# Two-layer hybrid diffusion block in one kernel: the last token strip is computed in blocks among the first steps of the mixers, and the second query pair is prepared in pieces between attention units

## What is computed

```python
u = adaln(x, norm1_w, shift, scale) @ w_in          # 2056 columns: pooling, SSD (Mamba-2), attention
pooled = pool_mixer(u[:, :256])                     # window means minus self, a small matmul
y_ssd  = ssd_bidirectional(u[:, 256:1288])          # chunks of 128 tokens, a state carried over the chunks, both ways
q, k, v = attn_split(u[:, 1288:])                   # 4 query heads and 2 key/value heads of 128
q, k = rmsnorm(q) * q_norm_w, rmsnorm(k) * k_norm_w
q, k = apply_axial_rope(q), apply_axial_rope(k)     # on the latent tokens
y_att = softmax(q @ k.T / sqrt(128)) @ v
x = x + gate * (concat([pooled, y_ssd, y_att]) @ w_out)
```

## Time and profile before

| what | value |
|---|---|
| median of 3 runs | 1600.78 us (1600.17 to 1602.5) |
| profiled execution | 1601.48 us |
| its span | 1599.7 us |
| TensorE busy | 1542.1 us, 96% |
| VectorE busy | 876.7 us, 55% |
| ScalarE busy | 592.0 us, 37% |
| GpSimd busy | 138.9 us, 9% |

### The profile page before, as it was taken

How to read it: one execution, slowest core, us unless ns; L and a number is a source line. 1 busy time by engine, 2 the same in 40 slices (tenths; PEclk the granted TensorE clock), 3 DMA queues, 4 the chain that set the end, 5 groups by cost and what they waited for, 6 DMA issues and landing times.

```text
span 1599.7 us, 22334 instructions
## 1 busy us (share of the span) xinstructions
PE 1542.1 (96%) x9086; PEld 1392.9 (87%) x9086; DVE 876.7 (55%) x1192; ACT 592.0 (37%) x896; POOL 138.9 (9%) x150
## 2 busy tenths in 40 slices
PE   6999879999999999999999999997999999999999
PEld 4899758899999999999999997985888788888887
DVE  4678777645765545555544367457656433333333
ACT  6634546634521111221122345354645322222223
POOL 0330132011000000000000024014101000000000
PEclk9999979999999999999999999998999999999999
DMA  9655300022444333333331123320013233333322
GB/s 370 177 171 170 86 1 2 1 67 90 134 145 131 112 126 132 106 131 132 122 115 56 50 79 84 81 69 1 1 53 93 86 92 99 92 92 97 91 85 83
DMA packets 204220, 156.05 MB, mean 98 GB/s; under 512 B 8740, under 2 KB 189804, under 8 KB 204012
## 3 DMA queue, kind: packets, MB, share of 16 engines
q1 hardware_dynamic: 202700, 150.16, 30.4%
q10 hardware_dynamic: 1440, 4.78, 0.8%
HBM read 151.52 MB, written 2.10 MB: 96 GB/s over the span
## 4 chain that ended last, share of the span: by engine, by line
PE 86%; DVE 7%; ACT 3%; issue 2%; POOL 1%; DMA 1%; SPq 0%; POOLq 0%; DVEq 0%; ACTq 0%
PE banks L1788 69%; PE banks L1906 5%; PE banks L2025 3%; PE banks L1932 2%; PE banks L2002 1%; DVE mod_sum L1249 1%; PE banks L2039 1%; DVE w_lo L1224 1%; PE banks L2063 1%; DVE nrm L1326 1%; PE banks L2003 1%; DVE h_lo L1320 1%; ACT nrm L885 1%; PE banks L1740 0%; PE banks L1727 0%
## 5 line engine op out<-in xcount | busy, mean ns | idle before, releaser
L1224 DVE TENSOR_TENSOR w_lo<-raw,w_hi 128x1056 fp32r<-128x1056 f32 x184 | 245.0, 1332 | 303.9 <-ACT w_hi L832 303.1
L1788 PE MATMUL banks<-h_hi,w_hi 128*128 128x384 f32 (+3 forms) x1296 | 386.4, 356 | 10.5 <-DVE h_lo L1320 5.4
L1788 PE MATMUL banks<-h_lo,w_hi 128*128 128x384 f32 (+3 forms) x1296 | 382.0, 353 | 0.0
L1788 PE MATMUL banks<-h_hi,w_lo 128*128 128x384 f32 (+3 forms) x1296 | 381.7, 353 | 0.0
L832 ACT ACTIVATE w_hi<-raw 128x1056 fp32r<-128x1056 f32 x184 | 198.5, 1079 | 247.2 <-PE banks L1788 227.1
L1788 PEld LDWEIGHTS banks<-h_hi,w_hi 128*128 128x128 f32 x1296 | 235.0, 188 | 40.9 <-DVE h_lo L1320 11.9
L1788 PEld LDWEIGHTS banks<-h_hi,w_lo 128*128 128x128 f32 x1296 | 237.2, 188 | 16.7
L1788 PEld LDWEIGHTS banks<-h_lo,w_hi 128*128 128x128 f32 x1296 | 237.0, 188 | 15.8
L1788 PE MATMUL banks<-g_hi,w_hi 128*128 128x384 f32 (+1 forms) x528 | 160.0, 357 | 0.0
L1788 PE MATMUL banks<-g_hi,w_lo 128*128 128x384 f32 (+1 forms) x528 | 159.1, 355 | 0.0
L1249 DVE SCALAR_TENSOR_TENSOR mod_sum<-mod_ring,cond,mod_sum 128x1024 f32<-128x1024 f32 x126 | 158.1, 1296 | 1.4
(11 more groups left out here) (209 smaller groups left out, 1871.0 us busy)
## 6 DMA issues: line engine op xcount, KB each, us to landing
raw<-in_w_dram SPq DMA_DIRECT2D x120, 512.0 KB, 3.8
mod_ring<-in_w_mod_dram SPq DMA_DIRECT2D x96, 512.0 KB, 4.8
raw<-in_w_in_dram SPq DMA_DIRECT2D x32, 512.0 KB, 4.8
raw<-in_w_out_dram SPq DMA_DIRECT2D x16, 512.0 KB, 3.7
raw<-in_w_dram SPq DMA_DIRECT2D x16, 384.0 KB, 3.1
x_in<-in_x_dram ACTq DMA_DIRECT2D x4, 512.0 KB, 7.4
out_dram<-x_out SPq DMA_DIRECT2D x8, 256.0 KB, 2.3
inv_n<-in_count_dram ACTq DMA_DIRECT2D x4, 400.0 KB, 3.1
```

Of the source, the lines that this page charges most:

```text
L1224: dve.tensor_tensor(w_lo[n % 2][:, :], raw[n % 4][:, :], as_f32(w_hi[n % 2][:, :]), ALU.subtract).then_inc(lo_ready, 1)
L1788: ins = pe.matmul(to(p, a, b), ws[:, w], xs(k, a, b), start=(first and q == 0), stop=(last and q == 2))
```

## The change

1. The second query pair's strip is no longer computed by `token_blocks` ahead of the mixers. It is cut into `block` events (six in layer 0, four in layer 1), each with the 24 matmuls of one block of tokens, placed among the transposes, `cs` and the first state steps. They use PSUM banks 0 and 1 in turn; the transposes now use banks 2 and 3 (one of them bank 0).
2. The transposes of the keys and of the first query head come after the last block, and the pooling matmuls after the first unit's scores. The first query pair's sum, scaling, sine and rotation are events `q01` among the blocks. The five state steps all stand in the head.
3. `x_w` moves to another address (on the ring of slabs), so that states can run before the last block; GpSimd now waits for the last modulation slab before the first `x_w` instead of before `h_prev`'s zeroes.
4. The second query pair's squares (`q23_squares`) are taken in the head, its sum in unit 0, its scaling in two halves, the sine, and the rotation's two steps in later units (`in_unit`). It gets tiles of its own (`qk_sq_last`, `rope_t_last`).
5. The SSD chunks begin at unit 1 (before: 2). The two last `mod_steps` of layer 0 and its `mod_total`/`mod_turn` are events too. Tile 16 of `w_out` is split at unit 8 (before: ahead of the mixers).

```diff
-        x_w = put("x_w", [P, 2, DIRS, 256], at=S0 + 19456)
+        x_w = put("x_w", [P, 2, DIRS, 256], at=M0 + 4 * TT * 256 + 8 * T)
...
-            ev = [("tr", "x", 0), ("tr", "x", 1), ("tr", "b", 0), ("tr", "k", 0), ("tr", "k", 1), ("cs",), ("q23", 0),
-                  ("pool", 0), ("pool", 1), ("q23", 1), ("tr", "q", 0)]
-            ev += states[:1] + [("q23", 2)] + states[1:2] + [("q23", 3)]
-            states = states[2:]
+            blocks = [("block", i, t) for i, t in enumerate(range(tok_from(l, 3), TT))]
+            ev = [("tr", "x", 0), blocks[0], ("cs",), ("q01", 0), ("tr", "x", 1), ("mod_steps",), blocks[1], ("tr", "b", 0), ("q01", 1), blocks[2]]
+            if l < DEPTH - 1:
+                ev += [("mod_total",), blocks[3], states[0], ("mod_turn",), blocks[4], states[1], ("q01", 2), states[2], ("q01", 3), blocks[5],
+                       ("tr", "k", 0), states[3], ("tr", "k", 1), ("tr", "q", 0), ("q23_squares",), states[4]]
+            else:
+                ev += [states[0], blocks[3], states[1], ("q01", 2), ("tr", "k", 0), states[2], ("q01", 3), ("tr", "k", 1), states[3],
+                       ("tr", "q", 0), ("q23_squares",), states[4]]
+            states = []
+            in_unit = {0: [("q23", 0), ("pool", 0), ("pool", 1)], 2: [("q23", 1)], 3: [("q23", 2)], 4: [("q23", 3)], 5: [("q23", 4)], 6: [("q23", 5)]}
+            if l == DEPTH - 1:
+                in_unit = {0: in_unit[0], 1: [("q23", 1)], 2: [("q23", 2), ("q23", 3)], 4: [("q23", 4)], 5: [("q23", 5)]}
+            in_unit[8] = [("w_out_tile",)]
...
+                ev += in_unit.get(u, [])
...
-                if todo and not states:
+                if todo and u:
                     last_c = todo.pop(0)
                     ev.append(("ssd", last_c))
-                for _ in range(2):
-                    if states:
-                        ev.append(states.pop(0))
...
-                for n in range(N_TOK):
+                for n in range(N_TOK - 1):
                     split_lo(base + N_FEAT + n + 1)
                     if n == 5:
                         rotate(0)
                     if l == 0:
                         biases(N_FEAT + n)
-                        mod_steps(N_FEAT + n)
+                        if n != 5:
+                            mod_steps(N_FEAT + n)
...
-                    for j in range(4):
+                    for j in range(4 if i == 0 else 2):
...
+                    elif e[0] == "block":
+                        i, t = e[1:]
+                        pe.wait_ge(tok_free, tok_count(l, 3) + (i - 1 if i >= 2 else i - 5))
+                        for half in range(2):
+                            n = base + N_FEAT + N_TOK - 2 + half
+                            pe.wait_ge(lo_ready, n + 1)
```

173 lines of the change are left out of this document (117 added, 56 removed).

## The result

The changed kernel took 1586.1 us (median of 4 runs, 1585.2 to 1588.0) against 1600.5 us before (4 runs, 1596.9 to 1602.5) in the same session: a ratio of 0.9915, 95% interval 0.9902 to 0.9929. The forecast was 1582.5 us with a range of 1573 to 1592. The profiled execution took 1585.9 us with a span of 1584.0 us; before these were 1601.5 and 1599.7 us.

What follows compares the result with a forecast made beforehand. TensorE was taken as the bound except in the two heads, idle there behind VectorE and GpSimd chains. 11.4 + 9.5 - 2 x 1.3 = 18.3 us off 1601.5 gave 1583.2, 1582.5 as median; range 1573 to 1592.

Steps and rivals of the forecast that it cites:

- The bound and the mechanism: Both heads: TensorE idles 15.7 and 10.6 us behind VectorE and GpSimd chains; blocks cover the first pair's, the second's moves out.
- Up to the first scores, layer 0: Layer 0's head: waits of 1.2 us for `w_lo` and `mod_total`, scores at 196.3, 1.4 us after TensorE is through.
- 1.0 us of contention: Each layer: allowance for GpSimd's sine and `x_w` beside VectorE's scaling and states; a full clash costs 1.9 us.
- The half clock for the pooling: Layer 0's head: pooling, 2.7 us at full clock, taken at half clock because the last dense block ended at 191.8.
- the layout: Step-by-step timing of both heads up to the first SSD output, in the profiled execution's time; gains 11.4 and 9.5 us.
- Layer 1: Layer 1's head: 2.1 us wait for the rotation, scores at 1081.7, `ssd_y` ends at 1098.5; gain 9.5 us.
- The pieces cost nothing: Units behind the heads: the second pair's scaling and rotation fit VectorE's roughly 2 us free per unit; costed at nothing.
- That rival, at 0.12: The pieces stretch the units: with all 10.5 us on the path the gain is 8, 1592.8 us; chance 0.12.
- Tile 16's split in unit 8 at nothing: Unit 8: the split, 1.25 us on VectorE and 1.07 on ScalarE, adds no time.
- Table switches: Both heads: 1.30 us per switch kept; rival at the page's higher price, 4 us more, 1586.5 us, chance 0.05.
- The dense heads: Rival: VectorE's chain stays hidden everywhere, all 26.3 us of idle time in the heads goes, 1574.5 us; chance 0.13.
- Slower by a clock that stays low: Rival: the low clock persists through the following units; with 30 us of additional work 1612 us; chance 0.03.

Runs made afterwards that it cites:

- fillers' run: Changed kernel plus unused matmuls: six in layer 1's wait for rotated queries, four ahead of the first `ssd_y` in both layers; 1588.5 us, ratio 0.9927.
- the run with the later chunk scan: Changed kernel with the SSD chunk pieces held back one unit, starting in unit 2 and not unit 1; 1590.1 us, ratio 0.9936.
- the run without the root: Changed kernel with the root of the second pair's normaliser replaced by a scaled copy, two table loads less per layer; 1584.8 us, ratio 0.9902.
- less scaling: Changed kernel with scaling of most heads of the second query pair left out, one head block per piece kept; 1587.8 us, ratio 0.9924.
- head 1's queries: Changed kernel with the transposes of head 1's queries issued at the start of the first attention unit in both layers; 1587.5 us, ratio 0.9922.
- sums first: Changed kernel with the two running-sum matmuls (`cs`) ahead of the last strip's first block instead of behind it; 1588.0 us, ratio 0.9926.

## Why the prediction was right, and where its steps were off

**The bound and the mechanism.** Right. The idle time of the heads lay behind VectorE's chains, the wait of 5.2 us for `x_w` is gone, and the two halves work as the text had it: undoing the pieces costs 18.9 us of stage, undoing the blocks 3 to 4 us. By stages, from the earlier trace rows and the starts above: layer 0 took 147.0 us from the strip to `w_out` (166.0 to 313.0) and takes 137.8, layer 1 114.7 (1059.5 to 1174.2) and takes 107.4. That is 9.2 + 7.3 = 16.5 us, where 10.1 + 8.2 = 18.3 were forecast. The spans differ by 15.7 us; most of the 0.8 us between is lost ahead of the strip of layer 0, which starts 0.7 us later. The forecast had the higher clock only inside its chain times, never as a term; by busy time it is over a third of what was won. The medians differ by 14.4 us, since the profiled execution of before lay 1 us above its median.

**Up to the first scores, layer 0.** The waits for `w_lo` and `mod_sum` were forecast at 1.2 us each and measured 1.4 and 1.3. Scores were to start 30.3 us after the strip's start and did at 32.3, with a wait of 1.29 us instead of 1.4. The term that was mis-sized is the scaling at 3.24 us, with 1.0 us of contention for the whole head. VectorE's rows and, below them, GpSimd's of the same stretch:

```profile
181.75 4.72 DVE L1489 SCALAR_TENSOR_TENSOR qk<-qk,qk_rt,qk_w 128x128 f32<-128x128 f32 x12
...
187.44 2.19 DVE L1615 TENSOR_TENSOR h_prev<-h_prev,decay_all 64x256 f32<-64x256 f32 x2
```

```profile
181.75 2.48 POOL L780 TENSOR_TENSOR x_w<-x_tok,w_state 128x256 f32<-128x256 f32 x4 [20.38 <-DVE b_tok L1591]
...
186.61 2.73 POOL L758 TENSOR_TENSOR rope_t<-qk,tab 128x512 f32<-128x512 f32 x2 [1.66 <-issue]
```

GpSimd waits for VectorE's copy of `b_tok`, and VectorE goes on to the scaling behind that same copy, so they collide from the first instruction: 1.5 us on the scaling (3.24 in the earlier trace rows), and 1.3 us on the state step beside the sine (0.87 us without it, last section). The two are 2.8 us where 1.0 was allowed.

**The half clock for the pooling.** Wrong place. Taking 5.1 us for the pooling was 2.3 us too much, and hid the error above: `ssd_y` ended 47.3 us after the strip's start where the layout has 47.2 us, or 48.5 with the 1.3 us of contention and semaphores that the sum adds. The half clock came afterwards, in the second SSD batch, for 1.45 us. That the head came out near the forecast is luck: two errors of some 2 us cancel, which only rows show.

**Layer 1.** The rotation wait was mis-sized, 3.2 us for 2.1, by the same collision, and the third `x_w` measured 1.3 us where 1.0 was forecast. The head ended 42.5 us after the strip's start, forecast 39.0 plus 1.3. The missing 2.2 us, and more, stand already at the first scores: forecast 22.2 us after the strip's start, measured 26.1. VectorE ended the rotation at 23.9 us where the layout has 21.2: the scaling took 2.55 us for 2.16, the state step beside the sine 2.31, the next one 1.27 and the rotation's second half 1.52 us. From there to the scores the layout has 1.0 us and the trace 2.2, largely because the transposes and the state ran at half clock. From the scores to the head's end the layout held: 16.8 us forecast, with 0.8 for a lower clock, and 16.4 measured, the new wait behind the queries' copy (2.13 us) included. TensorE stood at half clock for some 7 us; by the fillers' run the full clock would bring 1.2 us, and the rest goes to the wait for `h_prev`, where VectorE's chain bounds.

**The pieces cost nothing.** Right, and tested for the scaling: 7.29 us per unit before and 7.28 after, and 5.0 us less VectorE work, of the 10.5 us that the rival counted, brought nothing. For the rotation and the sine only the pace of the units speaks. That rival, at 0.12, fell.

**Tile 16's split in unit 8 at nothing.** The step that failed. The rows of ScalarE and VectorE in unit 8, and TensorE's below:

```profile
257.66 1.08 ACT L842 ACTIVATE w_hi<-raw 128x1056 fp32r<-128x1056 f32 x1
...
260.93 0.84 ACT L1142 ACTIVATE gn_sq<-mix 128x768 f32<-128x768 f32 x1 [2.19 <-DVE mix L1682]
```

```profile
258.77 1.26 DVE L1254 TENSOR_TENSOR w_lo<-raw,w_hi 128x1056 fp32r<-128x1056 f32 x1 [1.98 <-ACT w_hi L842]
259.95 0.95 DVE L1682 TENSOR_TENSOR mix<-mix,silu_z 128x768 f32<-128x768 f32 x1
```

```profile
261.83 1.50 PE L2146 MATMUL banks<-tab,gn_sq 128*128 128x1 f32 x12 [1.55 <-ACT gn_sq L1142]
```

VectorE stands 1.98 us for ScalarE's `w_hi`, then makes `w_lo`, and only then the product that becomes `gn_sq`, and the probabilities behind it. The kernel before shows no wait for `gn_sq`. I had counted the split's durations (1.25 and 1.07 us) against free time, and not VectorE's wait for ScalarE in between nor who is queued behind it. With the gated norm one unit later than the split, in the run with the later chunk scan, the wait was gone; that the split is the cause is read from these rows and from that run. The wait was 1.6 us as well with the second pair in the head and with most of its scaling out, so the pieces did not make it. The split itself was not moved alone.

**Table switches.** The step of 1.30 us per switch held: the load at 202.46 of the changed kernel was followed by its activation at 203.76. The Trainium skill, "ScalarE: Activation LUTs", What ACT_TABLE_LOAD costs, adds a drain of about 1.38 us to each switch. Two switches less per layer, in the run without the root, brought the first SSD output 0.9 us earlier in layer 0 and 1.4 us in layer 1, less than the two loads of 1.28 us themselves, so the drain does not show in this case. (With 4 us more, the prediction's 18.3 us would have become about 14, not the "near 15" that its text has; its 1586.5 us for that rival is right.)

**The other rivals.** The dense heads (1574.5) fell, because of what the text held against them: of the 16.6 us of idle time in the two heads, 12.3 us lie behind the last block. Slower by a clock that stays low fell: layer 0's clock was back at 217, and the units from 224.16 on kept their pace. That the 18.3 us of the sum came near owes something to luck as well. With one unit's work added back, layer 0's head gained 11.3 us where 10.1 were forecast and layer 1's 6.0 where 8.2 were. The units behind, put at nothing, lost 2.1 us net in layer 0 (where the half clock and the waits of 1.2 us at 221 and of 1.6 us for `gn_sq` stand) and gained 1.2 us in layer 1. The four differences make the missing 1.8 us.

## What to carry to other kernels

When a head has two chains in turn, laying dense work over the first only helps once the second is out of the way; moving the second away brought 10 us by itself. So cost both halves together and each by itself. When work is moved as "free", follow the waits inside it and the instructions queued behind it on each engine, not only its durations against free time. Once several chains end within 2 us of one another, removing one wait hands its time to the next: compare the stage and not the wait, and count the half-clock stretches in each stage, since one more of them hid a gain of 1.4 us here. Take a second profile of the same kernel before reading a stretch of low clock as the price of the place where it stands. A filler that costs nothing in a wait costs its full time where there is none.

## What the runs showed of the hardware

The half-clock stretch moves between executions of the same kernel: behind the first SSD output (214 to 217) in one, behind `gn_sq` (264 to 267) in the other, with waits of 1.7 and 1.6 us ahead of these places in both. Four variants had none in layer 0, two of them without fillers. In the first fillers' run it lasted from 261 to 268 and cost some 3 us, twice as much as in the others. In layer 1 the changed kernel had one 23 to 30 us after the stage's start in both its profiles. Four variants (less scaling, no root, head 1's queries, sums first) had another, some 40 us after that start, which it had in neither. What decides between the places stays open.

VectorE and GpSimd slow each other by what VectorE reads. In layer 1 the state step reading `h_prev` and `decay_all` took 2.31 us for two instructions beside GpSimd's sine and 0.87 us alone, while the step reading `h_prev` and a bank took 0.85 us beside GpSimd's `x_w` as well. VectorE's rows, then GpSimd's:

```profile
1066.03 2.31 DVE L1615 TENSOR_TENSOR h_prev<-h_prev,decay_all 64x256 f32<-64x256 f32 x2
1068.37 0.85 DVE L1623 TENSOR_TENSOR h_prev<-h_prev,banks 64x256 f32<-64x256 f32 x2
...
1076.83 0.87 DVE L1615 TENSOR_TENSOR h_prev<-h_prev,decay_all 64x256 f32<-64x256 f32 x2
```

```profile
1065.36 2.69 POOL L758 TENSOR_TENSOR rope_t<-qk,tab 128x512 f32<-128x512 f32 x2 [1.14 <-issue]
1068.02 2.69 POOL L780 TENSOR_TENSOR x_w<-x_tok,w_state 128x256 f32<-128x256 f32 x4
```

The Trainium skill, "SBUF — State Buffer", Who interferes with whom, says that a VectorE instruction with two inputs in SBUF contends with a GpSimd instruction that reads SBUF, and that one with at most one such input, outside its two-port modes, does not. The trace agrees with both halves: 2.31 against 0.87 us, and 0.85 us in either place.
